# Three experts of a routed feed-forward layer: plain fp32 products replaced by three passes of rounded high and low parts

## What is computed

```python
def _swiglu(x, w_gu, w_down, f):
    gu = x @ w_gu
    return (jax.nn.silu(gu[..., :f]) * gu[..., f:]) @ w_down

def _moe_ffn(x, router, w_gu, w_down):
    logits = (x @ router).astype(jnp.float32)
    top_v, top_i = lax.top_k(logits, TOP_K)
    ...
    for e in range(N_EXPERTS):
        y = y + gate[..., e:e + 1] * _swiglu(x, w_gu[e], w_down[e], D_FF_EXPERT)
    return y
```

## Time and profile before

| | us |
|---|---|
| median of three runs | 2637.31 (2636.81 to 2639.85) |
| profiled execution, own time | 2641.07 |
| its span, first to last instruction | 2639.3 |
| PE busy in the span | 2380.0 (90%) |
| expert 0 (208 columns), first product to first product of expert 1 | 107.01 |
| expert 1 (192 columns) | 98.95 |
| expert 2 (168 columns) | 87.13 |

### The profile page before, as it was taken

How to read it: one execution, slowest core, us unless ns; L and a number is a source line. 1 busy time by engine, 2 the same in 40 slices (tenths; PEclk the granted TensorE clock), 3 DMA queues, 4 the chain that set the end, 5 groups by cost and what they waited for, 6 DMA issues and landing times.

```text
span 2639.3 us, 42728 instructions
## 1 busy us (share of the span) xinstructions
PE 2380.0 (90%) x17150; PEld 2264.9 (86%) x17150; DVE 898.8 (34%) x1468; ACT 540.3 (20%) x1022; POOL 985.0 (37%) x1397
## 2 busy tenths in 40 slices
PE   8998789899999987999999788889599999999993
PEld 8988768899999977998989778867599999999993
DVE  3684323311011267566666533413301000000004
ACT  2351221310011033222333211321200000100103
POOL 4557525688888845233333005535100000000001
PEclk9999899899999998899999768899689999999996
DMA  7214441222222222111121102541255677788884
GB/s 288 98 64 151 147 178 62 96 87 80 89 83 90 74 81 75 43 59 51 59 59 59 35 18 88 184 153 65 101 191 185 213 241 242 231 267 272 273 283 161
DMA packets 98648, 348.06 MB, mean 132 GB/s; under 512 B 13504, under 2 KB 18752, under 8 KB 93616
## 3 DMA queue, kind: packets, MB, share of 16 engines
q1 hardware_dynamic: 73136, 279.08, 31.5%
q10 hardware_dynamic: 19328, 45.18, 5.0%
q0 software_dynamic: 6016, 21.43, 2.3%
HBM read 319.19 MB, written 26.47 MB: 131 GB/s over the span
## 4 chain that ended last, share of the span: by engine, by line
PE 63%; issue 15%; DVE 10%; POOL 5%; DMA 4%; ACT 3%; ACTq 0%; POOLq 0%; DVEq 0%; SPq 0%
PE ps L550 25%; PE ps L1138 14%; PE ps L1153 8%; PE ps L788 4%; POOL wl L472 3%; DMA raw<-weights 3%; POOL wh L468 2%; PE ps L651 1%; DVE x L1762 1%; PE ps L1000 1%; PE ps L996 1%; PE ps L979 1%; PE ps L655 1%; PE ps L835 1%; DVE x L1750 1%
## 5 line engine op out<-in xcount | busy, mean ns | idle before, releaser
L468 POOL TENSOR_TENSOR wh<-raw,tab 128x256 fp32r<-128x256 f32 x672 | 438.8, 684 | 898.0 <-PE ps L550 603.1
L472 POOL TENSOR_TENSOR wl<-raw,wh 128x256 fp32r<-128x256 f32 x672 | 518.6, 803 | 0.0
L1138 PE MATMUL ps<-work,raw 128*128 128x128 f32 (+6 forms) x3072 | 424.2, 299 | 13.2 <-DMA raw<-weights 10.8
L1138 PEld LDWEIGHTS ps<-work,raw 128*128 128x128 f32 x3072 | 419.5, 191 | 16.7 <-issue 5.1
L550 PE MATMUL ps<-xh,wh 128*128 128x272 f32 x2048 | 314.4, 305 | 56.4 <-POOL wl L472 13.1
L550 PEld LDWEIGHTS ps<-xh,wh 128*128 128x128 f32 x2048 | 284.3, 200 | 70.0 <-issue 20.8
L550 PE MATMUL ps<-xh,wl 128*128 128x272 f32 x2048 | 303.5, 299 | 0.0
L550 PEld LDWEIGHTS ps<-xh,wl 128*128 128x128 f32 x2048 | 281.7, 198 | 1.8 <-issue 0.5
L550 PE MATMUL ps<-xl,wh 128*128 128x272 f32 x2048 | 279.8, 288 | 0.0
L550 PEld LDWEIGHTS ps<-xl,wh 128*128 128x128 f32 x2048 | 264.9, 188 | 0.0
L519 POOL DMA_DIRECT2D rows_y<-moe_h x8 | 4.3, 540 | 656.9 <-DVE moe_h L2243 656.9
(11 more groups left out here) (375 smaller groups left out, 3071.3 us busy)
## 6 DMA issues: line engine op xcount, KB each, us to landing
raw<-weights SPq DMA_DIRECT2D x488, 512.0 KB, 3.7
moe_h<-cache SPq DMA_DIRECT2D x6, 2048.0 KB, 9.6
moe_h<-cache ACTq DMA_DIRECT2D x4, 2048.0 KB, 13.9
work<-cache SPq DMA_DIRECT2D x4, 2048.0 KB, 9.8
moe_h<-rows_x POOLq DMA_DIRECT2D x14, 512.0 KB, 7.5
rows_x<-lnsq ACTq DMA_DIRECT2D x9, 512.0 KB, 11.0
work<-scratch ACTq DMA_DIRECT2D x16, 272.0 KB, 4.2
work<-cache ACTq DMA_DIRECT2D x2, 2048.0 KB, 10.9
```

Of the source, the lines that this page charges most:

```text
L468: nc.gpsimd.tensor_tensor(flat(h1[:, k0:k1]), flat(r1[:, k0:k1]), one_col, MUL).then_inc(pool_hi, 1)
L472: low = nc.gpsimd.tensor_tensor(flat(l1[:, k0:k1]), flat(r1[:, k0:k1]), flat(h1[:, k0:k1]).bitcast(F), SUB)
L1138: last = mm(ps[:, j // 2, (j % 2) * c:(j % 2 + 1) * c], raw[:, slot % RAW, k, :], M_x[:, r % 2, k, 0:c], start=(k == 0), stop=(k == KT - 1))
```

## The change

`FINE = (0, 1, 2)`: the products of the first three experts (208, 192 and 168 columns) are made in three passes of rounded parts. The other five stay plain.

- Weights: ACT rounds each 128 x 1024 tile into one of six high buffers (`weight_high`), DVE subtracts it from `raw` into one of six low buffers (`weight_low`); two of the six are the old `wh` and `wl`, four lie in `xh` and `xl`, whose contents are no longer wanted. Both run four tiles (`LEAD`) ahead of PE. 108 tiles in all.
- Activations: ACT copies the turned rows out of PSUM in rounded form, DVE makes the low part (`rows_low`); of each hidden tile ACT makes the high part (`hidden_high`) and DVE the low part (`hidden_low`).
- PE makes high x high, high x low, low x high for each product, and waits for the split of a tile instead of its landing; before the down phase it waits for the last low hidden tile.
- SP loads a new tile into `raw` when the tile in it has been split, not when it has been multiplied. It reads the flag `over` first.

```diff
+FINE = (0, 1, 2)
+HALVED, LEAD = 6, 4
...
+            def halved(g):
+                if g // 36 in FINE:
+                    sp.wait_ge(split_l, KT + fine_slots(g) + 1)
+                else:
+                    multiplied(g)
...
+                def weights(q):
+                    slot = e36 + q
+                    if fine:
+                        pe.wait_ge(split_l, KT + nf + q + 1)
+                    else:
+                        pe.wait_ge(w_in[slot % RAW], 16 * (slot // RAW + 1))
+
+                def product(out, q, k, plain, ah, al, start, stop):
+                    if not fine:
+                        return mm(out, raw[:, (e36 + q) % RAW, k, :], plain, start=start, stop=stop)
+                    i = (nf + q) % HALVED
+                    mm(out, E_h[i][:, k, :], ah, start=start, stop=False)
+                    mm(out, E_h[i][:, k, :], al, start=False, stop=False)
+                    return mm(out, E_l[i][:, k, :], ah, start=False, stop=stop)
...
-                pe.wait_ge(m_h, e12 + FT)
+                if fine:
+                    pe.wait_ge(f_hl, (HALVES + nf // 36 + 1) * FT)
+                else:
+                    pe.wait_ge(m_h, e12 + FT)
...
+            def weight_high(g):
...
+                act.wait_ge(w_in[slot % RAW], 16 * (slot // RAW + 1))
+                if i >= HALVED:
+                    act.wait_ge(w_used, S_MOE + (g - HALVED if fine_slots(g - HALVED) == i - HALVED else g) + 1)
+                else:
+                    act.wait_ge(w_used, S_MOE)
+                s(A(E_h[i % HALVED], raw[:, slot % RAW], ACT.Copy), split_h, KT + i + 1)
...
+                def hidden_high(f):
+                    act.wait_ge(m_h, e12 + f + 1)
+                    s(A(M_hh[:, f, 0:c], M_hp[:, f % 2, 0:c], ACT.Copy), f_hh, (HALVES + nf // 36) * FT + f + 1)
                 for f in range(FT):
+                    weight_high(36 * r + 2 * f + LEAD)
+                    weight_high(36 * r + 2 * f + 1 + LEAD)
...
+            def weight_low(g):
...
+                dve.wait_ge(split_h, KT + i + 1)
+                s(V.tensor_tensor(E_l[i % HALVED], raw[:, (S_MOE + g) % RAW], E_h[i % HALVED].bitcast(F), SUB), split_l, KT + i + 1)
+
+            def rows_low(r):
...
+                    dve.wait_ge(m_xe, KT // 2 * r + i + 1)
+                    s(V.tensor_tensor(M_xl[:, r % 2, 2 * i:2 * i + 2, 0:c],
...
+                def hidden_low(f):
+                    dve.wait_ge(f_hh, nh + f + 1)
+                    s(V.tensor_tensor(M_hl[:, f, 0:c], M_hp[:, f % 2, 0:c], M_hh[:, f, 0:c].bitcast(F), SUB), f_hl, nh + f + 1)
```

More of the change, by code:

```diff
@@ L66, with fine_slots @@
 NTAB = _n
+def fine_slots(g):
+    return 36 * sum(r in FINE for r in range(g // 36)) + (g % 36 if g < NE * 36 and g // 36 in FINE else 0)
 class Serial:
@@ L347, in trunk @@
         M_tri = tk(P)
-        M_x, M_h = tk(2, KT, CMAX), tk(FT, CMAX)
+        rounded = lambda v: bass.AP(work_r, v.offset, v.ap)
+        M_x, M_h, M_l = tk(2, KT, CMAX), tk(FT, CMAX), tk(FT, CMAX)
+        M_xh, M_hh, M_hl = rounded(M_x), rounded(M_h), rounded(M_l)
+        M_xl = x_r[:, 0:2 * KT * CMAX].rearrange("p (a b c) -> p a b c", a=2, b=KT)
+        E_h, E_l = ([w[:, j] for j in range(SPLIT)] + [flat(v)[:, j * KT * P:(j + 1) * KT * P].rearrange("p (a b) -> p a b", b=P)
+                                                      for j in range(HALVED - SPLIT)] for w, v in ((wh, xh), (wl, xl)))
         C_st, C_mv, C_rs, C_nb = tk(NT, 12), tk(NT, 2), tk(NT, 1), tk(NT, 1)
@@ L438, in _, with expert_weights, multiplied @@
                     turns(S_KV1[3], 4, 28, None, W_KV1 + 12)
-            sp.wait_ge(r_dve, ORDER)
-            for r in range(NE):
+            def expert_weights(r, lo, hi, free):
                 e = sp.value_load(R_ki[0:1, r:r + 1], min_val=0, max_val=NE - 1)
-                for q in range(36):
+                for q in range(lo, hi):
                     slot = S_MOE + 36 * r + q
                     j = slot % RAW
-                    sp.wait_ge(w_used, slot + 1 - RAW)
+                    free(36 * r + q - RAW)
                     sp.dma_start(raw[:, j:j + 1, :, :], I["weights"][ds(e * 36 + (W_MOE + q), 1)].rearrange(
                         "o p (k c) -> p o k c", k=KT)).then_inc(w_in[j], 16)
+            def multiplied(g):
+                sp.wait_ge(w_used, S_MOE + g + 1)
+            def halved(g):
[3 more added lines that the diff above has]
+                    multiplied(g)
+            sp.wait_ge(r_dve, ORDER)
+            expert_weights(0, 0, RAW, multiplied)
+            sp.wait_ge(r_dve, COUNTED)
+            over = sp.value_load(R_over[0:1, 0:1], min_val=0, max_val=1)
+            with sp.If(over > 0):
+                for r in range(NE):
+                    expert_weights(r, 0 if r else RAW, 36, multiplied)
+            with sp.Else():
+                for r in range(NE):
+                    expert_weights(r, 0 if r else RAW, 36, halved)
+            sp.end_ifs()
             sp.wait_ge(out_done, 16 * N_OUT)
@@ L1670, in expert @@
                     s(A(M_s[:, f % 2, 0:c], ps[:, f % 2, 0:c], ACT.Silu), m_silu, e12 + f + 1)
+                    if fine and f:
+                        hidden_high(f - 1)
+                if fine:
+                    hidden_high(FT - 1)
+                q = 24
                 if r + 1 < NE:
@@ L1673, in expert @@
                 for d in range(KT):
+                    while q < 24 + ((d + 1) * FT + KT - 1) // KT:
+                        weight_high(36 * r + q + LEAD)
+                        q += 1
                     evict(r, d)
@@ L1718, in _ @@
                 s = Serial(act, act_chain2)
+                for g in range(LEAD):
+                    weight_high(g)
                 expert_rows(0)
@@ L2253, in expert @@
+                if r + 1 < NE and r + 1 in FINE:
+                    rows_low(r + 1)
+                q = 24
                 for d in range(KT - 1):
+                    while q <= 24 + ((d + 1) * FT + FT // 2) // KT:
+                        weight_low(36 * r + q + LEAD)
+                        q += 1
                     turned(r, d)
+                while q < 36:
+                    weight_low(36 * r + q + LEAD)
+                    q += 1
             over = dve.value_load(R_over[0:1, 0:1], min_val=0, max_val=1)
@@ L2275, in _ @@
                 s = Serial(dve, dve_chain2)
+                for g in range(LEAD):
+                    weight_low(g)
+                if 0 in FINE:
+                    rows_low(0)
                 for r in range(NE):
```

62 lines of the change are left out of this document (46 added, 16 removed).

## The result

The changed kernel takes 2647.4 us (median of 7 runs, 2646.39 to 2660.96), the kernel before 2637.31 (7 runs, 2631.31 to 2641.25): ratio 1.0051, 95% interval 1.0029 to 1.0073. That is slower by 0.5%, +13.4 us by the ratio (7.6 to 19.3), +10.1 by the two medians; the forecast was +10.9 and 2648.2. The profiled execution took 2647.4 us, its span is 2645.6.

A forecast was written before the change was run, and what follows sets the result against it. PE's matmuls were taken to bound the three experts' 293.1 us. Terms 11.6 + 0.8 + 0.9 - 2.4 = +10.9 us on the median 2637.3 gave 2648.2 us, slower by 0.4%; range 2636 to 2687.

The forecast's parts named there:

- The 2592 matmuls: Experts 0 to 2 on PE: loads set the pace at 111.7 ns per rounded matmul, 96.5 us an expert, +11.6 us.
- rounded matmuls keep 125 ns: Rival on PE: 125 ns is the rounded form's own price at any width, +46.1 us, 2682.7 us; chance 0.17.
- streaming binds: Rival on PE: loads hide wholly and columns cost 0.46 ns each, -52.4 us, about 2584 us; chance 0.11.
- The fall back to plain passes: Rival on PE: each of three passes costs a whole plain product, +555.8 us, some 3192 us; chance 0.08, falling clock included.
- The fall of the clock: Counted with the fall back rival (0.08 together): PE's clock drops to 1.2 GHz because the array streams less of the time.
- Splits and ends of up phases: ACT and DVE splits have cover, costing nothing; PE waits 0.3 us at each of three up phase ends, +0.9 us.
- The weights' waits: PE's three waits for weights go, as buffers free at the split: -2.4 us (between -2.4 and 0).
- The start: Before the first product PE also waits for the low rows; only the last subtraction sticks out, +0.8 us.
- The order of transfers: SP frees buffers at the split, four tiles ahead of PE, so the tile queue is deeper: -2.4 us.
- POOL's list is the same: Remark in the step on transfers: POOL's instructions do not change; no cost was put on them.

The follow-up runs named there:

- half_load: The changed kernel, but second and third pass load only the first 64 of 128 weight columns and write only 64 partitions: 2618.47 us (one execution).
- narrow64: The changed kernel, but second and third pass multiply only the first 64 columns, every weight load as it was: 2789.05 us (one execution).
- hold: The changed kernel, but SP loads the fifth and later weight tiles only when the first rows are transposed: 2646.28 us, ratio 1.0031 to the kernel before.

## Why the prediction was right, and where it was not

**The 2592 matmuls.** Right. Forecast 111.7 ns, measured 111.5 to 111.7; experts of one length, forecast about 102 us, measured 101.76, 100.16, 100.03. The reason given (a load of 128 weights sets the pace) is shown by three runs together: fewer columns changed nothing at the upper level, shorter loads did, and a shared load did. The Trainium skill, page "TensorE: Matmul & The Clock Gate", section "LDWEIGHTS (loading the stationary operand)", has 106.7 ns for such a load by its formula; the trace has 111.6. Over 2592 matmuls these 4.9 ns are 12.7 us, about as much as the whole effect of the change.

**The rivals on PE.** That rounded matmuls keep 125 ns fell (`half_load`: it was the stream). That streaming binds fell by the equal distances; the fast load of the Trainium skill, same page, section "Weight-path perf modes", does not show for rounded weights, at 111.6 ns a load no quicker than plain ones (111.3 and 111.7). The fall back to plain passes fell too. The fall of the clock did not come with the change, 0.98 to 1.00, but the reason given against it was weak: two microseconds of 4-column matmuls say little about it, and `narrow64` shows such a fall with every weight load as it was in the change.

**Splits and ends of up phases.** Right: PE never waited for a weight tile; the ends of the three up phases cost 0.2 us on PE and 1.0 on its loads, forecast 0.9 in all.

**The weights' waits.** -2.4 came as forecast in experts 0 to 2. Of the later experts, PE waited 9.9 us for weights against 8.7 before; they ended 0.7 us longer, within the 1 to 2 us named.

**The start: the term that was mis-sized.** Forecast +0.8, measured +5.84. The step that failed is "The order of transfers": it took the buffers that SP gets back at the split as a gain alone. It named the queue of loaded tiles as deeper and never asked what else is on the way when the additional loads are issued. It is the moment of PE's longest wait for a DMA here, 25.1 us for the rows before and 29.7 after, and the four more tiles are loaded in it. Of the +5.84, this is 3.70, POOL's longer wait. The two rest terms are smaller: the low rows, the 0.8 of the forecast, measured 1.26, since all four subtractions on DVE, about 0.61 us each, take longer than ACT's copies of 0.54 and fall behind them, not only the last one. And POOL's scatter, for which the prediction had nothing ("POOL's list is the same"), took 0.87 longer. `hold`, which takes the early loads away, has a start of +0.68, near the 0.8 by luck: there POOL's wait is 1.34 shorter than before, and that hides most of the others.

**The sum.** The experts came to +8.86 (forecast 11.6 + 0.9 - 2.4 = 10.1), the start to +5.84, the rest to +0.7: 15.4 in the profiled executions against 10.9 forecast. The experts came in 1.2 under their forecast, the start 5.0 over its own. That the two medians, +10.1 apart, lie closer to the forecast is luck: the interval of the ratio, 7.6 to 19.3 us, holds both. The direction, and the reason for it, did not hang on the start.

**Left open:** on which resource scatter and weight loads meet (engines of the DMA, DRAM or a queue) was not told apart; why POOL's scatter instructions take longer beside the splits, and why the clock fell in `narrow64`, stayed open; nor was it measured within 0.2% what the wait on SP is worth for the whole kernel.

## What to carry to other kernels

Price a pass by the longer of its stream and its load. Here, at the upper level of the clock, three rounded passes of one load each cost 3 x 111.6 = 335 ns a product whatever the width, against 2 x 0.85 ns a column for plain ones (the 176.7 of 208 columns in the earlier trace rows), so by this estimate they win only above 335 / 1.70 = 197 columns (192 lost 1.21 us, 208 gained 5.25); where two passes share a load, the same numbers put that at 111.6 / (1.70 - 2 x 0.46) = 143 columns, an estimate that was run at 168 and above only. And where an edit frees buffers earlier, look up what the earlier loads then run beside.

## What the runs showed of the hardware

The granted clock of TensorE can fall to the lower level with PE busy all the time (`narrow64`, from 2195 us). It stayed low there for 116 us. And a load shorter than the stream beside it shows no cost: of the pair of 336 and 168 columns only one of two loads shows, 265 ns against 266 worked out from one load and the wide stream.
